# Block 2's first feed-forward on unscaled tokens, with the inverse root applied at the relu, and the grid attention's query weights sent behind the feed-forward's units

## The reference, cut to what matters

```python
def rmsnorm(x, g):
    y = xf * lax.rsqrt(jnp.mean(xf * xf, axis=-1, keepdims=True) + EPS_2)
    return y * g
...
for layer in range(DEPTH):
    u = rmsnorm(h, attn_norm_g[layer])
    mix = ab_mixer(u, ...) if layer % 2 == 0 else c_mixer(u, w_qkv_c, ...)
    h = h + mix
    u = rmsnorm(h, mlp_norm_g[layer])
    h = h + jnp.square(jax.nn.relu(u @ w_ff1[layer])) @ w_ff2[layer]
```

## Time and profile before

| | us |
|---|---|
| median of 3 runs | 1644.88 |
| lowest and highest of them | 1644.49, 1651.28 |
| profiled execution, its own time | 1646.0 |
| its span in the profile | 1644.2 |
| TensorE busy in the span | 1554.3 |
| VectorE busy | 802.4 |
| ScalarE busy | 552.2 |

### The profile page before, as it was taken

How to read it: one execution, slowest core, us unless ns; L and a number is a source line. 1 busy time by engine, 2 the same in 40 slices (tenths; PEclk the granted TensorE clock), 3 DMA queues, 4 the chain that set the end, 5 groups by cost and what they waited for, 6 DMA issues and landing times.

```text
span 1644.2 us, 23827 instructions
## 1 busy us (share of the span) xinstructions
PE 1554.3 (95%) x9655; PEld 1115.4 (68%) x9657; DVE 802.4 (49%) x1710; ACT 552.2 (34%) x1015; POOL 0.5 (0%) x7
## 2 busy tenths in 40 slices
PE   7998999999999999999989989989999989899999
PEld 5856745453486774545448667878999964599897
DVE  6897721111334671111136376684665537565544
ACT  3444311111224531111132455413444322644443
POOL 0000000000000000000000000000000000000000
PEclk9999999999999999999999989899999999999999
DMA  9531689999943368999990000217444544013552
GB/s 325 195 128 46 220 347 429 428 428 428 355 173 121 112 226 347 429 428 429 426 362 20 1 1 2 105 41 267 154 159 148 204 154 153 1 52 114 194 204 77
DMA packets 83728, 346.65 MB, mean 211 GB/s; under 512 B 8240, under 2 KB 15280, under 8 KB 71360
## 3 DMA queue, kind: packets, MB, share of 16 engines
q1 hardware_dynamic: 76272, 338.28, 52.6%
q10 hardware_dynamic: 7376, 7.26, 1.4%
HBM read 344.48 MB, written 1.05 MB: 210 GB/s over the span
## 4 chain that ended last, share of the span: by engine, by line
PE 42%; DVE 4%; ACT 2%; DMA 1%; issue 1%; DVEq 0%; ACTq 0%
PE ps L820 41%; DVE ring L2425 2%; DMA ring<-in_w_ff 1%; PE ps L1340 1%; DVE ring L2431 0%; DVE arena L2926 0%; ACT ring L2206 0%; DVE ring L2428 0%; DVE small L2928 0%; PE ps L1565 0%; DVE arena L2428 0%; DVE ring_r L2425 0%; DVE arena L2425 0%; ACT ring L2208 0%; ACT y_r L1808 0%
## 5 line engine op out<-in xcount | busy, mean ns | idle before, releaser
L820 PE MATMUL ps<-ring,arena 128*64 128x512 f32 (+6 forms) x1728 | 378.7, 573 | 19.2 <-DMA ring<-in_w_up 11.4
L820 PEld LDWEIGHTS ps<-ring,arena 128*64 128x64 f32 (+2 forms) x1728 | 134.0, 141 | 244.6 <-issue 237.3
L820 PE MATMUL ps<-arena_r,ring_r 128*128 128x272 f32 (+1 forms) x896 | 255.7, 285 | 0.0
L1808 ACT ACTIVATE arena<-ps 128x512 f32<-128x512 f32 (+7 forms) x161 | 73.3, 479 | 374.3 <-PE ps L820 177.3
L820 PEld LDWEIGHTS ps<-arena_r,ring_r 128*128 128x128 f32 x896 | 168.6, 188 | 0.0
L820 PE MATMUL ps<-arena_r,y_r 128*128 128x272 f32 (+1 forms) x560 | 157.5, 287 | 4.6 <-ACT arena L2346 2.4
L820 PE MATMUL ps<-h_r,y_r 128*128 128x272 f32 (+1 forms) x528 | 150.4, 285 | 0.0
L820 PE MATMUL ps<-arena_r,ff_hi_r 128*128 128x272 f32 (+1 forms) x576 | 119.7, 290 | 1.4 <-DVE hT L2425 1.4
L2431 DVE SCALAR_TENSOR_TENSOR arena<-arena,small,ps 128x512 f32<-128x512 f32 x16 | 12.0, 748 | 214.5 <-PE ps L820 214.5
L2425 DVE TENSOR_TENSOR ring_r<-ring,y_r 128x1024 fp32r<-128x1024 f32 x74 | 88.9, 1222 | 44.5 <-ACT y_r L1808 44.5
L820 PEld LDWEIGHTS ps<-arena_r,y_r 128*128 128x128 f32 x560 | 104.6, 189 | 6.7 <-ACT arena L2346 2.9
(11 more groups left out here) (329 smaller groups left out, 2246.4 us busy)
## 6 DMA issues: line engine op xcount, KB each, us to landing
ring<-in_w_gate SPq DMA_DIRECT2D x32, 2048.0 KB, 15.8
ring<-in_w_up SPq DMA_DIRECT2D x32, 2048.0 KB, 17.2
ring<-in_w_down SPq DMA_DIRECT2D x32, 2048.0 KB, 13.3
ring<-in_w_ff SPq DMA_DIRECT2D x32, 2048.0 KB, 9.2
ring<-in_w_in SPq DMA_DIRECT2D x8, 2048.0 KB, 19.7
ring<-in_w_in_ab SPq DMA_DIRECT2D x5, 2048.0 KB, 12.7
ring<-in_w_o SPq DMA_DIRECT2D x4, 2048.0 KB, 10.3
ring<-in_ple_gate SPq DMA_DIRECT2D x4, 2048.0 KB, 8.5
```

What stands on the lines that cost most here:

```text
L820: return pe.matmul(o, lhsT, rhs, start=a, stop=z)
L1808: return act.activation(o, i, ACT.Copy, scale=scale)
```

## The change

For layer 0 of block 2 the feed-forward's first product is made on `R` x gain, without the root. ScalarE makes the high part straight from `R` with the gain as scale (`gained_high`), and VectorE the low part (`gained_low`); the low parts of the first four groups go to another buffer, `edge`, because the projection still reads the old one. The root is applied in the relu, max(x, 0) x root, which moves from ScalarE to VectorE in every chunk. The eight mean-square sums leave the projection and stand between the third and the fourth `hidden` unit. The fillers are gone. PSUM banks are dealt anew. SP issues the two halves of the query weights of `w_qkv_c` behind both loads of chunk 0 and no longer ahead of them. Layer 1 keeps its form.

```diff
-        edge_t = sb("edge_t", 2048 + NEDGE * DIFF_H)
+        edge_t, edge_r = sb_pair("edge", 2048 + NEDGE * DIFF_H)
...
-        MS_BANK = [7, 7, 0, 7]
+        MS_BANK = [7, 4, 0, 7]
...
+        FF_LO = [[edge_lo[:, c, :] for c in range(4)] + [uT_lo[:, c, :] for c in range(4, KC)], [uT_lo[:, c, :] for c in range(KC)]]
...
-        OUT_BANK = [1, 3, 5, 6, 0, 2, 4, 1]
+        OUT_BANK = [list(range(KC)), [1, 3, 5, 6, 0, 2, 4, 1]]
...
-                    for half in range(2):
-                        sp.dma_start(slot(4 + half, KC), cols_of("w_qkv_c", half * 512, 512)).then_inc(slot_full[4 + half], 16)
                     sp.wait_ge(wo_mm, 4)
                     ff_load(L, 0, 0, 0)
                     sp.wait_ge(wo_mm, 8)
                     ff_load(L, 0, 1, 0)
+                    for half in range(2):
+                        sp.dma_start(slot(4 + half, KC), cols_of("w_qkv_c", half * 512, 512)).then_inc(slot_full[4 + half], 16)
...
-                        if c == 7 and u == 4:
+                        if c == 7 and u == 4 and L == 1:
...
-                    if u >= 4:
-                        mean_square(2 * L + 1, u - 4)
-                for c in range(4, KC):
-                    mean_square(2 * L + 1, c)
-                if L == 0:
-                    stay_busy(5, 7)
-                else:
+                    if u >= 4 and L == 1:
+                        mean_square(3, u - 4)
+                if L == 1:
+                    for c in range(4, KC):
+                        mean_square(3, c)
                     residual_in()
...
                     hidden(FF_UNITS[L] + q, q, 0, q, 0)
+                    if L == 0 and q == 2:
+                        pe.wait_ge(res_ev, KC)
+                        for c in range(KC):
+                            mean_square(1, c)
...
+                            if first and q == 4:
+                                pe.wait_ge(rs_ready, 2)
...
 # ScalarE
-                    act.wait_ge(f1_ev, j * 4 + (32 * L + 4))
-                    act.wait_ge(f1_mm, j * 4 + (32 * L + 4))
-                    act.activation(rl[d][:, :, 0:n], ps[:, 0:4, 0:n], ACT.Relu).then_inc(f1_relu, 4)
+                    if L == 1:
+                        ...
...
+                def gained_high(c):
+                    act.wait_ge(res_ev, c + 1)
+                    act.activation(uT_hi[:, c, 0:n], R[:, c, 0:n], ACT.Copy, scale=mlp_g[:, 0, c:c + 1]).then_inc(uT_hi_ev, 1)
+
+                if L == 0:
+                    for q in range(4):
+                        gained_high(2 * q)
+                        gained_high(2 * q + 1)
+                        first_high_part(q)
+                        if q == 1:
+                            for c in range(4):
+                                residual_squares(c)
+                    for c in range(4, KC):
+                        residual_squares(c)
...
                 for U, m, dd, q, ahead in ff_units(L, 0, 0, False)[:2]:
                     high_part(U, m, dd, q, ahead)
+                if L == 0:
+                    inverse_root(1)
                 squares_of_relu(0, 0)
...
 # VectorE
                 def squares_of_relu(j, d):
+                    if L == 0:
+                        dve.wait_ge(f1_mm, j * 4 + 4)
+                        stt(rl[d], ps[:, 0:4, 0:LT], 0.0, rs_t.unsqueeze(1).to_broadcast([P, 4, LT]), ALU.max, ALU.mult).then_inc(f1_relu, 4)
...
+                def gained_low(c):
+                    dve.wait_ge(res_ev, c + 1)
+                    dve.wait_ge(uT_hi_ev, 4 + c + 1)
+                    stt(FF_LO[0][c], R[:, c, :], mlp_g[:, 0, c:c + 1], uT_hi[:, c, :].bitcast(F32), ALU.mult, ALU.subtract).then_inc(uT_ev, 1)
...
+                for c in range(4):
+                    mixed_in(c)
+                out_low(L, 7)
+                if L == 0:
+                    for q in range(4):
+                        if q == 2:
+                            for c in range(4, KC):
+                                mixed_in(c)
+                        gained_low(2 * q)
+                        gained_low(2 * q + 1)
+                        first_low_part(q)
...
+                if L == 0:
+                    dve.wait_ge(rs_ready, 2)
                 squares_of_relu(0, 0)
```

More of the change, by code:

```diff
@@ L1670, in _ @@
                 for c in range(A_H):
-                    ins = pe.transpose(ps[:, 2 * t, c * rows(t):(c + 1) * rows(t)], oacc[0:rows(t), t, c * P:(c + 1) * P], ident[0:rows(t), 0:rows(t)])
+                    ins = pe.transpose(ps[:, 4 + t, c * rows(t):(c + 1) * rows(t)], oacc[0:rows(t), t, c * P:(c + 1) * P], ident[0:rows(t), 0:rows(t)])
                 ins.then_inc(yT_mm, 1)
@@ L1685, in hidden @@
                             mm(o, hi[:, e, c], uT_hi[:, k, 0:FF_N[L]], k == 0, False)
-                            ins = mm(o, hi[:, e, c], uT_lo[:, k, 0:FF_N[L]], False, False)
+                            ins = mm(o, hi[:, e, c], FF_LO[L][k][:, 0:FF_N[L]], False, False)
                             if e == 1 and f == 3:
@@ L1768, in _ @@
                     if i == 0:
-                        pe.wait_ge(uT_full, 2 * KC + k + 1)
+                        pe.wait_ge(uT_full, KC + k + 1)
                     ins = mm(ps[0:rows(t), 4 + i % 4, :], uT[:, k, cols(t)], slot(s, KC)[:, k, :], k == 0, k == KC - 1)
@@ L2342, in squares_of_relu @@
                 def squares_of_relu(j, d):
-                    act.wait_ge(f1_ev, j * 4 + (32 * L + 4))
-                    act.wait_ge(f1_mm, j * 4 + (32 * L + 4))
-                    act.activation(rl[d][:, :, 0:n], ps[:, 0:4, 0:n], ACT.Relu).then_inc(f1_relu, 4)
+                    if L == 1:
+                        act.wait_ge(f1_ev, j * 4 + (32 * L + 4))
+                        act.wait_ge(f1_mm, j * 4 + (32 * L + 4))
+                        act.activation(rl[d][:, :, 0:n], ps[:, 0:4, 0:n], ACT.Relu).then_inc(f1_relu, 4)
                     act.wait_ge(f1_relu, j * 4 + (32 * L + 4 + 4))
@@ L2362, in feed_forward, with residual_squares @@
                     out_high(L, u)
-                for c in range(KC):
+                def residual_squares(c):
                     act.wait_ge(res_ev, KC * L + c + 1)
                     squares(2 * L + 1, c)
[L2366 to L2372, removed]
+                def gained_high(c):
[11 more added lines that the diff above has]
+                        residual_squares(c)
+                else:
+                    for c in range(KC):
+                        residual_squares(c)
+                    first_high_part(0)
+                    inverse_root(3)
+                    for c in range(KC):
+                        act.wait_ge(uT_full, 2 * KC + c + 1)
+                        copy(uT_hi[:, c, 0:n], uT[:, c, 0:n]).then_inc(uT_hi_ev, 1)
+                        if c in (1, 3, 5):
+                            first_high_part((c + 1) // 2)
                 for U, m, dd, q, ahead in ff_units(L, 0, 0, False)[:2]:
                     high_part(U, m, dd, q, ahead)
+                if L == 0:
+                    inverse_root(1)
                 squares_of_relu(0, 0)
@@ L3268, in _ @@
                 dve.wait_ge(yT_mm, t + 1)
-                tt(uT[:, 0:A_H, cols(t)], ps[:, 2 * t, 0:A_H * rows(t)].rearrange("p (c s) -> p c s", c=A_H), tzT[:, :, cols(t)], ALU.mult).then_inc(yT_ev, 1)
+                tt(uT[:, 0:A_H, cols(t)], ps[:, 4 + t, 0:A_H * rows(t)].rearrange("p (c s) -> p c s", c=A_H), tzT[:, :, cols(t)], ALU.mult).then_inc(yT_ev, 1)
                 if t > 0:
@@ L3307, in first_low_part, with mixed_in @@
                     low_part(FF_UNITS[L] + q, q, 0, q)
+                def mixed_in(c):
+                    dve.wait_ge(wo_mm, KC * L + c + 1)
+                    tt(R[:, c, 0:N], R[:, c, 0:N], ps[:, OUT_BANK[L][c], 0:N], ALU.add).then_inc(res_ev, 1)
+                def gained_low(c):
+                    dve.wait_ge(res_ev, c + 1)
+                    dve.wait_ge(uT_hi_ev, 4 + c + 1)
+                    stt(FF_LO[0][c], R[:, c, :], mlp_g[:, 0, c:c + 1], uT_hi[:, c, :].bitcast(F32), ALU.mult, ALU.subtract).then_inc(uT_ev, 1)
@@ new lines, in feed_forward @@
+                if L == 0:
[6 more added lines that the diff above has]
+                        first_low_part(q)
+                else:
+                    for c in range(4, KC):
+                        mixed_in(c)
+                    first_low_part(0)
+                    dve.wait_ge(rs_ready, 2 * L + 2)
+                    scaled(2 * L + 1, mlp_g[:, L, :], 0)
+                    for c in range(KC):
+                        if c + 1 < KC:
+                            scaled(2 * L + 1, mlp_g[:, L, :], c + 1)
+                        dve.wait_ge(uT_hi_ev, (4 + KC) * L + 4 + c + 1)
+                        tt(uT_lo[:, c, 0:N], uT[:, c, 0:N], uT_hi[:, c, 0:N].bitcast(F32), ALU.subtract).then_inc(uT_ev, 1)
+                        if c in (1, 3, 5):
+                            first_low_part((c + 1) // 2)
```

3 lines of the change are left out of this document (2 added, 1 removed).

## The result

The changed kernel takes 1638.59 us, the median of 7 runs (1636.80 to 1640.57), against 1648.08 for the kernel before in the same comparison (7 runs, 1644.49 to 1651.28). The ratio is 0.9941, with a 95% interval of [0.9927, 0.9955], so 0.59% faster. The forecast of 1638.4 us holds. The class is less clear: I had given 0.80 to "within 0.5%" and 0.16 to "faster by over 0.5%". The ratio lies past that bound, but its interval reaches to 0.9955 and doesn't exclude the other side. Of the profiled execution, the time fell from 1646.0 to 1638.59 us and the span from 1644.2 to 1636.8, so by 7.4 us.

A forecast was written before the change was run, and what follows sets the result against it. Bound: a late weight transfer after the output projection, its wait filled with constant matmuls. Removed 9.10 + 1.28, kept or added 3.70 + 0.21, net 6.47 us off median 1644.88: 1638.4 us; 8-in-10 range 1634.5 to 1643.5.

The forecast's parts named there:

- Step 1: First feed-forward unit's weight load: still issued at 1116.47, it lands 7.5 us later, at 1124.0.
- the bound: Later landing kept for that load: 1125.4, if its full 7.5 us began only at 1117.9.
- Steps 2 and 3: Projection to first four feed-forward units: first unit starts at 1128.44 without gap, margin 2.1 us; later margins at least 2.4.
- Rival A: Thin cover: first unit's load or the copies end late, each later microsecond costing one; time 1642.1 us, chance 0.12.
- Step 4: Eight sums between third and fourth unit cost TensorE 3.7 us; the root is hidden by 2.1 us.
- Step 5: Relu on VectorE takes 1.29 us; pause ahead of chunk 1 grows from 1.21 to 1.42 us; loop covers the rest.
- Rival C: Slower: relu not covered in the loop; gain gone at a relu of 2.85 us, 1653 at 4.0; chance 0.04.
- my formula: If the relu takes e more than 1.29 us, each of seven loop chunks waits e - 0.64.
- Step 6: Later transfers on SP's queue, query weights included, and the changed banks delay nothing: all free.
- rival B: More comes back, at the loop's 1.48 us exit gap or restarts: 2 us more gained, 1636.4 us, chance 0.13.
- Rival D: Slower: without fillers, a load after 1130 idles TensorE and the clock drops to 1.2 GHz; about 1655 us, chance 0.02.
- Rival E: Nothing moves: something other than load and root held the first unit; 1644 to 1646 us, chance 0.03.

The follow-up runs named there:

- late-load kernel: Changed kernel with the first feed-forward load issued two projection units later: 1647.42 us, ratio 0.9999 to the kernel before.
- double relu: Changed kernel with a second VectorE operation of the same kind and size ahead of each relu: 1648.19 us, ratio 1.0003 to the kernel before.
- one part alone: Kernel before with only the new queue order, query weights behind both chunk-0 loads: 1645.2 us, ratio 0.9985; stretch 47.29 us against 48.23.
- the other lost 4.7: Changed kernel with the old queue order, so unscaled tokens and no fillers: 1649.71 us, ratio 1.0008 to the kernel before; stretch 52.93 us.
- A fill of constants: Changed kernel with the first load two projection units later and six constant matmuls in TensorE's pause: 1645.37 us, ratio 0.9985 to the kernel before.

## Why the prediction was right, and where it was not

*Step 1, the load.* Right: forecast 7.5 us from issue to landing, measured 7.9, between 7.5 and the bound. The 6.8 us worked out from the Trainium skill (DMA: Bandwidth & Descriptors, anatomy of one DMA) were too short for this load. The section gives its figures for transfers issued by GpSimd, and these come from SP.

*Steps 2 and 3, no gap.* Right. The first unit follows the projection at once, the margin is 1.7 us instead of 2.1, and the late-load kernel measured it by using it up. ScalarE's high parts with the gain take 0.51 us each and not 0.42, which the margins absorbed. Rival A did not come. But its price, one for one, was too low: the clock adds to it.

*Step 4, the sums.* Right in size: 12 units of 3.02 us make 36.3 of the 40.02, which leaves 3.7. The root is finished at 1140.54 + 0.43 = 1140.97 and wanted at 1143.1, the forecast 2.1 us later. What I treated as a price to be paid was avoidable on an idle engine.

*Step 5, the relu.* 1.29 us, as taken. The pause is 1.49 us for 1.42 forecast, and in the loop the cover holds. Rival C did not come, but its price was wrong. I put the loss of the whole gain at a relu of 2.85 us. That sum leaves out the pause ahead of chunk 1, which grows by the full extra time, and the clock behind the pauses. The double relu occupies VectorE for 2.6 us in a chunk, for which my formula still leaves 1.9 us of gain (6.47 - 7 x 0.65); measured, the gain was gone (ratio 1.0003).

*Step 6, the queue behind.* Right: the query transfers follow at 1127.74, and no wait for a transfer stands in the chain up to the loop's end.

*The sum.* 6.47 forecast, 6.73 and 6.83 measured in the stretch (41.50 against 48.23 and 48.33). The mechanism and the terms hold. Two terms were missing. The loop is 0.44 us shorter, where I said it would stay at 169.7; rival B named more gain, but at the loop's exit, where the issue gap is 1.52 us for 1.48 before, so not that one. And the profiled executions differ by 7.4 us, while the means of all runs taken, 79 of before at 1647.8 and 13 of after at 1638.5, differ by 9.3. The traces of before and after account for 6.7 + 0.44, about 7.2. **Some 2.1 us remain open.** Both profiled executions of the kernel before (1646.0 and 1645.34) are faster than its mean, by about that much. Stages whose code is the same vary widely: the projection starts between 1102.5 and 1107.9 us in these traces, and the grid attention's stage takes between 85.2 and 87.5, in kernels of before and after alike. The granted clock differs there from one execution to the next. From the end of the scan stage to the projection, the kernel before took 40.5 us at a granted clock of 0.92 in one trace and 37.7 at 1.00 in the other, more of a difference than the open part. I found no stage that is systematically shorter by 2.1 us.

*The class, and the luck in the time.* The 0.80 for "within 0.5%" rested on 1644.88 us, the median of three runs, which lay at the low end of what the kernel before does (later medians 1649.0, 1647.5, 1647.26). I subtracted 6.5 us from that low median and so kept the forecast inside 0.5%. Over all runs the difference is 9.3 of 1647.8 us, 0.57%. That the time I gave, 1638.4, was met to 0.2 us is luck: the baseline was 3 us too low and the difference 3 us too small. With a spread of 2.3 us from run to run (one standard deviation), a forecast 1.7 us from the class bound deserved a chance much nearer to even than five to one.

*Rival D, the clock.* It didn't come here, but the runs give it a larger weight than I did. The clock fell behind each of the pauses of 2.66 to 8.50 us that the experiments opened, two of them made by a longer relu and not by a late load.

*Rival E* is excluded by the chain.

## What to carry to other kernels

When two chains end close together, price an edit against the latest of them: here one part alone gave 0.9 us, the other lost 4.7, and the two together gained 6.7. After removing a wait, look whether the filler that bridged it is now the bound. Before opening a pause on TensorE, add to it what the clock takes behind it. A fill of constants returned that part (2.4 of 8.7 us), not the pause itself. And sums of squares that stand on TensorE's path can be added up beforehand on an engine that idles there: it was worth 3.2 us for 2.5 us of VectorE's idle time.

## What the runs showed of the hardware

The clock's price is paid behind the pause and grows less than the pause does. At 0.50, against 1.00, TensorE lost 1.7 us after a pause of 2.66 and 1.5 to 1.7 after 2.75, 1.5 after 3.28, 2.4 after 5.98, and 2.7 after 8.50, each in one trace; after 1.49 none. A matmul of 272 columns then starts every 0.227 us instead of 0.126.

The price of one and the same pause can differ between executions. The grid attention has a pause of 2.51 us in all fourteen traces. In eight of them the clock falls to 0.50 behind it, in six it doesn't, and the kernel before shows both (first trace, second trace):

```profile
1391.89 2.10 PE L820 MATMUL ps<-arena 128*128 128x272 f32 x8 [2.51 <-ACT arena L1808]
```
```profile
1390.31 3.79 PE L820 MATMUL ps<-arena 128*128 128x272 f32 x8 [2.51 <-ACT arena L1808]
```

So a loss behind a pause of this length, read from one trace, is what it cost that time.

The loop's 1344 matmuls take 169.73 to 169.75 us in the kernels with scaled tokens and 169.28 to 169.29 in those with unscaled ones (the double relu apart). What sets this is open; most of the difference lies in matmuls whose buffers are the same in both.
